# Moving the modulation sums of an adaptive-norm block out of the first attention and into the feed-forward and convolution stages

## What is computed

```python
x = x + attention(rmsnorm(x, attn_norm_g)) @ w_out           # 8 forgetting heads, 8 stick-breaking heads
u = causal_dwconv(rmsnorm(x, ffn_norm_g) @ w_up, conv_w, conv_b)
x = rmsnorm(x + (silu(gate(u)) * val(u)) @ w_down, final_norm_g)
sc = silu(c)
for i in range(2):
    mod = sc @ w_ada[i] + b_ada[i]                             # 1024 x 6144, for one row vector
    sh_m, sc_m, g_m, sh_f, sc_f, g_f = jnp.split(mod, 6, axis=-1)
    h = rms_norm(x, norm_mix[i]) * (1 + sc_m) + sh_m
    y = moba_attention(h) if i == 0 else short_conv(h, w_in, conv_w, w_out)
    x = x + g_m * y
    h = rms_norm(x, norm_ffn[i]) * (1 + sc_f) + sh_f
    x = x + g_f * swiglu(h, w_gate_up[i], w_down[i])
```

## Time and profile before

| | |
|---|---|
| median of 3 runs | 1031.73 us (1027.55 to 1032.73) |
| the profiled execution | 1032.79 us, of which the span is 1030.9 us |
| PE busy | 988.2 us, 96% of the span |
| DVE busy | 720.3 us, 70% |
| ACT busy | 484.0 us, 47% |
| mean granted TensorE clock | 0.969 |
| the 48 modulation steps on DVE (line 797) | 112.6 us, mean 2345 ns |

### The profile page before, as it was taken

One profiled execution on the slowest core, in us unless ns is written; L12 is line 12 of the kernel. 1 busy time (PEld: TensorE's weight loads), 2 busy tenths in 40 slices (PEclk: granted clock), 3 DMA queues, 4 the chain that ended last, 5 costly groups with the idle time before them and its releaser, 6 DMA issues.

```text
span 1030.9 us, 18959 instructions
## 1 busy us (share of the span) xinstructions
PE 988.2 (96%) x7553; PEld 959.3 (93%) x7553; DVE 720.3 (70%) x939; ACT 484.0 (47%) x696; POOL 45.2 (4%) x78
## 2 busy tenths in 40 slices
PE   5899987999999999999999999999999989999998
PEld 5899877999999999989999999999999989999876
DVE  5699884778788867888675677787666665555544
ACT  4245543556566334655454444433444454444531
POOL 4100000000000100001000001010000000000000
PEclk8999997999999997999989999999899999999999
DMA  9678473365554982646645688798265626455441
GB/s 319 219 234 304 173 264 110 111 196 163 174 195 170 385 300 60 227 163 222 231 131 194 211 284 279 247 365 283 91 198 168 199 85 201 165 197 169 165 162 41
DMA packets 131064, 207.60 MB, mean 201 GB/s; under 512 B 4686, under 2 KB 109504, under 8 KB 124864
## 3 DMA queue, kind: packets, MB, share of 16 engines
q1 hardware_dynamic: 122784, 156.44, 45.5%
q0 software_dynamic: 6912, 50.33, 13.8%
q10 hardware_dynamic: 1312, 0.04, 0.1%
HBM read 205.74 MB, written 1.05 MB: 201 GB/s over the span
## 4 chain that ended last, share of the span: by engine, by line
PE 85%; DVE 8%; ACT 3%; issue 2%; DMA 1%; SPq 1%; ACTq 0%; DVEq 0%
PE bank L1276 25%; PE bank L1277 25%; PE bank L1278 25%; PE bank L1356 2%; PE bank L1312 2%; DVE w_lo L782 2%; PE bank L1314 2%; PE bank L1317 1%; ACT w_hi L466 1%; SPq L377 1%; DMA v_in<-in_conv_w 1%; DVE ada_acc L797 1%; DVE scr L815 0%; ACT prob L727 0%; DMA k_fox<-sb_l 0%
## 5 line engine op out<-in xcount | busy, mean ns | idle before, releaser
L782 DVE TENSOR_TENSOR w_lo<-w_raw,w_hi 128x1024 fp32r<-128x1024 f32 x294 | 356.3, 1223 | 213.2 <-ACT w_hi L466 209.3
L466 ACT ACTIVATE w_hi<-w_raw 128x1024 fp32r<-128x1024 f32 x294 | 306.6, 1054 | 308.6 <-PE bank L1278 286.6
L1276 PE MATMUL bank<-act_hi,w_hi 128*128 128x256 f32 x1440 | 411.3, 286 | 1.1 <-DVE act_lo L1096 1.1
L1277 PE MATMUL bank<-act_lo,w_hi 128*128 128x256 f32 x1440 | 408.5, 284 | 0.0
L1278 PE MATMUL bank<-act_hi,w_lo 128*128 128x256 f32 x1440 | 408.4, 284 | 0.0
L1276 PEld LDWEIGHTS bank<-act_hi,w_hi 128*128 128x128 f32 x1440 | 276.3, 192 | 1.9 <-issue 1.7
L1277 PEld LDWEIGHTS bank<-act_lo,w_hi 128*128 128x128 f32 x1440 | 276.3, 192 | 0.3 <-issue 0.2
L1278 PEld LDWEIGHTS bank<-act_hi,w_lo 128*128 128x128 f32 x1440 | 276.1, 192 | 0.0
L797 DVE SCALAR_TENSOR_TENSOR ada_acc<-ada_raw,silu_c,ada_acc 128x2048 f32<-128x2048 f32 x48 | 112.6, 2345 | 2.2 <-DMA ada_raw<-in_w_ada 1.9
L1277 PE MATMUL bank<-hid_lo,w_hi 128*128 (+1 forms) x352 | 99.5, 283 | 0.0
L1276 PE MATMUL bank<-hid_hi,w_hi 128*128 (+1 forms) x352 | 99.2, 282 | 0.0
(11 more groups left out here) (248 smaller groups left out, 1297.5 us busy)
## 6 DMA issues: line engine op xcount, KB each, us to landing
ada_raw<-in_w_ada POOLq DMA_DIRECT2D x48, 1024.0 KB, 5.3
w_raw<-in_w_gate_up SPq DMA_DIRECT2D x44, 1024.0 KB, 5.1
w_raw<-in_w_down SPq DMA_DIRECT2D x33, 1024.0 KB, 5.0
w_raw<-in_w_in SPq DMA_DIRECT2D x24, 1024.0 KB, 5.3
w_raw<-in_w_up SPq DMA_DIRECT2D x22, 1024.0 KB, 5.1
w_raw<-in_w_qkv SPq DMA_DIRECT2D x12, 1024.0 KB, 7.0
w_raw<-in_w_out SPq DMA_DIRECT2D x8, 1024.0 KB, 5.2
w_raw<-in_w_o SPq DMA_DIRECT2D x4, 1024.0 KB, 5.9
```

The source lines that it names most:

```text
L466: act.activation(unit(w_hi, u), raw_half(c, h), ACT.Copy).then_inc(hi_ready, 1)
L782: dve.tensor_tensor(unit(w_lo, u), raw_half(c, h), unit(w_hi, u).bitcast(F32), ALU.subtract).then_inc(lo_ready, 1)
L1276: pe.matmul(dst, a_hi, b_hi, start=start, stop=False, skip_group_check=True)
L1277: pe.matmul(dst, a_hi, b_lo, start=False, stop=False, skip_group_check=True)
```

## The change

The 16 steps that stood in and behind the first attention are taken out of it, but for two that stand at its end. Six go into UP1 (pairs 1, 3, 4, 6, 8 and 9), the next eight into DOWN1, the following 24 into the second attention, UP2 and DOWN2, and the last eight into IN3, one behind each of its first eight chunks. The first two fetches of POOL move behind its fills of the padded tiles. `PIECES` gets an eighth piece, and three pieces (2, 4 and 6) are folded into the norms 4, 5 and 6, between `rstd` and the first use of the gain. On PE, the sums of piece 5 now stand between IN3 and OUT3. DVE's code for UP1 is written out for all 11 pairs instead of a loop.

```diff
-ADA_AT1 = [(1, 0), (1, 1), (2, 1), (3, 1), (4, 0), (4, 1), (5, 1), (6, 1), (7, 0), (7, 1), (9, 0), (10, 1), (11, 1),
-           (12, 0), (12, 1)]
+ADA_OUT1, ADA_UP1, ADA_IN3 = 2, (1, 3, 4, 6, 8, 9), 40
...
-PIECES = ((0, 0, 15), (0, 16, 31), (0, 32, 47), (1, 0, 15), (1, 16, 31), (1, 32, 39), (1, 40, 47))
+PIECES = ((0, 0, 15), (0, 16, 31), (0, 32, 39), (0, 40, 47), (1, 0, 15), (1, 16, 31), (1, 32, 39), (1, 40, 47))
+ACC_READ = (1, 2, 4)
...
                         for n in range(3):
                             pool.memset(ada_acc[:, n, :], 0.0).then_inc(ada_zero, 1)
-                        fetch(0)
-                        fetch(1)
...
                                 pool.memset(pad[64 * (1 - half):64 * (2 - half), half:8:2, :], value).then_inc(pad_set, 1)
+                        fetch(0)
+                        fetch(1)
...
                 link(dve.scalar_tensor_tensor(rstd[:], n_t[:], 1.5, n_y[:], ALU.add, ALU.mult))
+                if piece is not None:
+                    modulation(piece)
...
+                    if c0 == UP1 and p in ADA_UP1:
+                        ada(ADA_OUT1 + ADA_UP1.index(p))
                     gated_pair(c, pair, p, i, convolve)
...
-                    if (c, h) in ADA_AT1:
-                        ada(ADA_AT1.index((c, h)))
...
-            for n in range(len(ADA_AT1), 16):
+            for n in range(ADA_OUT1):
                 ada(n)
...
-            modulation(0)
-            gated_layer(UP1, 0, 1, True)
-            down_layer(DOWN1, 16, None)
+            gated_layer(UP1, 0, PAIRS, True)
+            down_layer(DOWN1, 8, None)
...
-            modulation(4)
             for c in range(12):
...
+                if c < 8:
+                    ada(ADA_IN3 + c)
             split(OUT3 + 2)
             split(OUT3 + 3)
+            modulation(5)
             add_up(OUT3, lambda k: mod[:, 1, G_M + k:G_M + k + 1])
-            modulation(5)
...
@@ PE @@
                 for h in range(2):
                     out1_chunk(n, h)
             square_sums(1)
-            mod_sums(0)
...
             square_sums(4)
+            mod_sums(2)
             mod_sums(3)
...
+            mod_sums(5)
             for n in range(4):
                 for h in range(2):
                     output_chunk(OUT3, n, h, lambda k: ot_hi[:, k, :], lambda k: ot_lo[:, k, :],
                                  lambda k: pe.wait_ge(sc_lo, k // 2 + 1) if k % 2 == 0 else None)
-            mod_sums(5)
             square_sums(6)
             mod_sums(6)
+            mod_sums(7)
```

More of the change, by code:

```diff
@@ L799, in _, with norm @@
             ada_step = [4]
-            def norm(n, gain, shift=None, version=None, late=None):
+            def norm(n, gain, shift=None, version=None, late=None, piece=None):
                 if late is not None:
@@ L906, in gated_layer @@
                     step(c0 + 2 * p, pair0 + p, p, None)
+                if straight == PAIRS:
+                    return
                 ada_step[0] = 2
@@ L1144, in _ @@
             split_unit(UP1 + 1, 1)
+            gated_layer(UP1, 0, PAIRS, True)
+            down_layer(DOWN1, 8, None)
+            norm(2, lambda k: vcol(0, V_FINAL + k), version=3, late=(QKV + 1, 0))
             modulation(0)
-            gated_layer(UP1, 0, 1, True)
-            down_layer(DOWN1, 16, None)
-            norm(2, lambda k: vcol(0, V_FINAL + k), version=3, late=(QKV + 1, 0))
-            modulation(1)
             norm(3, lambda k: gain2[:, 0, k:k + 1], shift=lambda k: mod[:, 0, SH_M + k:SH_M + k + 1])
             split_unit(QKV + 1, 1)
-            modulation(2)
+            modulation(1)
             def head_mean(n):
@@ L1219, in _ @@
             add_up(OUT2, lambda k: mod[:, 0, G_M + k:G_M + k + 1])
-            norm(4, lambda k: gain2[:, 1, k:k + 1], shift=lambda k: mod[:, 0, SH_F + k:SH_F + k + 1], late=(UP2 + 1, 0))
+            norm(4, lambda k: gain2[:, 1, k:k + 1], shift=lambda k: mod[:, 0, SH_F + k:SH_F + k + 1], late=(UP2 + 1, 0),
+                 piece=2)
             split_unit(UP2 + 1, 1)
             modulation(3)
-            gated_layer(UP2, PAIRS, 3, False, ADA + 8)
-            down_layer(DOWN2, ADA + 16, lambda k: mod[:, 0, G_F + k:G_F + k + 1])
-            norm(5, lambda k: gain2[:, 2, k:k + 1], shift=lambda k: mod[:, 1, SH_M + k:SH_M + k + 1], late=(IN3 + 1, 0))
+            gated_layer(UP2, PAIRS, 3, False, ADA)
+            down_layer(DOWN2, ADA + 8, lambda k: mod[:, 0, G_F + k:G_F + k + 1])
+            norm(5, lambda k: gain2[:, 2, k:k + 1], shift=lambda k: mod[:, 1, SH_M + k:SH_M + k + 1], late=(IN3 + 1, 0),
+                 piece=4)
             split_unit(IN3 + 1, 1)
-            modulation(4)
             for c in range(12):
@@ L1260, in _ @@
                                       ALU.subtract).then_inc(sc_lo, 1)
+                if c < 8:
+                    ada(ADA_IN3 + c)
             split(OUT3 + 2)
             split(OUT3 + 3)
+            modulation(5)
             add_up(OUT3, lambda k: mod[:, 1, G_M + k:G_M + k + 1])
-            modulation(5)
-            norm(6, lambda k: gain2[:, 3, k:k + 1], shift=lambda k: mod[:, 1, SH_F + k:SH_F + k + 1], late=(UP3 + 1, 0))
+            norm(6, lambda k: gain2[:, 3, k:k + 1], shift=lambda k: mod[:, 1, SH_F + k:SH_F + k + 1], late=(UP3 + 1, 0),
+                 piece=6)
             split_unit(UP3 + 1, 1)
-            modulation(6)
+            modulation(7)
             gated_layer(UP3, 2 * PAIRS, 1, False)
@@ L1639, in _ @@
             square_sums(2)
+            mod_sums(0)
+            square_sums(3)
             mod_sums(1)
-            square_sums(3)
-            mod_sums(2)
             def head_sums(n):
@@ L1651, in head_sums @@
                 else:
-                    pe.wait_ge(mod_done, 3)
+                    pe.wait_ge(mod_done, 2)
                 if n % 2 == 0:
```

4 lines of the change are left out of this document (2 added, 2 removed).

## The result

The changed kernel takes 1041.58 us (median of 4 runs, 1039.90 to 1044.52) against 1032.23 us (4 runs, 1027.55 to 1032.78): a ratio of 1.0119, 95% interval 1.0085 to 1.0152. It is slower: by 9.4 us between the medians, by 12 us by the ratio, whose interval is 8.8 to 15.7 us. The profiled execution took 1042.26 us, with a span of 1040.6 us and a mean granted clock of 0.966 (before 1030.9 and 0.969).

The account below looks back on a forecast made before the run. PE was taken as the bound, busy throughout UP1 and IN3, waiting little in the first attention. Added 10.0 us less 5.4 saved gave +4.6, stated as 1036.3 us; own range 1034 to 1039, 80% range 1030 to 1042.

Parts of the forecast that it names:

- the largest chance, 0.51: Whole kernel: chance given to a time the same as before, within about 0.5% (5.2 us).
- What the change takes away: First 184 us: four items (start, forget sums' wait, clock behind it, small waits) save 5.4 us.
- The start: Kernel start: small vectors land earlier with the fetches behind the fills, saving 0.8 us (bounds 0.5 and 1.05).
- the wait with its clock: First attention: PE's wait for the forget sums' moved rows goes, 2.3 us, and the half clock behind it, 1.2.
- The small waits: First attention: steps ahead of the first `o_tok` (0.4) and two `sb_t` (0.6, 0.2) go, taken as 1.1 us.
- The clock behind piece 5: Behind piece 5, after IN3: one-column products let PE's clock fall, costing 1.0 us (bounds 0 and 1.7).
- the clock holds: Rival, chance 0.15: piece 5 costs only its columns, with no clock loss, giving 1035.3 us.
- The second sums of norms 4 and 6 lie before the next `act_hi`: Norms 4 and 6: the second eight columns of sums end before `act_hi`, so no cost was added for them.
- The norms: Norms 4 and 6: the folded modulation between `rstd` and `scr` costs 0.5 us each.
- UP1 and IN3: Added steps make DVE late for PE: 2.0 us in UP1 (pairs 4 and 9, 1.0 each), 2.7 in IN3.
- DVE becomes the bound: Rival, chance 0.17: lateness carries on, UP1 costs 6.5 and IN3 5.6 us, +7.4, giving 1043.7 us.
- Norm 5: Norm 5: PE's 16 columns end late and the modulation follows, so `scr` comes 1.6 us later.

Follow-up runs that it names:

- e2: Kernel before with the accumulation at chunk (1, 0) taken out of the first attention, fetches unmoved: 1028.30 us, ratio 0.9971.
- e1: Kernel before with only POOL's first two 1 MB fetches moved behind its pad fills: 1027.41 us, ratio 0.9971.
- e11: Kernel before with 16 extra one-column products, the same as piece 5's, between IN3 and OUT3, result unused: 1039.49 us, ratio 1.0087.
- e12: Kernel before with eight extra f32 products of 256 columns between IN3 and OUT3, result unused: 1034.14 us, ratio 1.0043.
- e3: Changed kernel with UP1's six accumulations cut to 64 of 2048 columns, transfers unchanged: 1039.11 us, ratio 1.0080.
- e4: Changed kernel with IN3's eight accumulations cut to 64 of 2048 columns, transfers unchanged: 1037.08 us, ratio 1.0062.
- e5: Changed kernel with pieces 3 and 7 summed into bank 5 instead of bank 7: 1037.19 us, ratio 1.0067.
- e13: Changed kernel with the edits of e5 and e6, and UP1's six steps at pairs 0, 2, 4, 6, 8, 10: 1030.39 us, ratio 0.9995.
- e6: Changed kernel with piece 5 cut into four parts of four columns, ahead of the waits of IN3's chunks 6 to 9: 1033.98 us, ratio 1.0044.
- e7: Changed kernel with piece 5 cut into four parts of four columns, behind OUT3's first four half chunks: 1037.43 us, ratio 1.0076.
- e8: Kernel before with both small edits, later first fetches and no accumulation at chunk (1, 0): 1027.42 us, ratio 0.9975.

## Why the prediction was wrong

Its sign of the sum was right, its size was not: +4.6 us forecast, +9.7 in the profiled executions, 9.4 by the medians. The median, 1041.58 us, lies just inside the 80% range of 1030 to 1042 and outside the forecast's own 1034 to 1039, and the largest chance, 0.51, stood on a difference within 0.5%.

**What the change takes away** was read rightly. The start was 0.7 for 0.8 and the wait with its clock 4.1 for 3.5. e2 shows that the step at (1, 0) is the cause, as the forecast had it, and e1 that the fetches at the start act on the start alone. The small waits were 0.9 for 1.1 (the forecast's three terms of 0.4, 0.6 and 0.2 add up to 1.2): the one of 0.6 gave 0.9, the other two nearly nothing. Another 1.4 us is clock, which no step of the forecast held, and which is this pair of executions and not the change.

**The clock behind piece 5** is the step that failed. It took one stretch of 3.5 us from the earlier trace rows, bounded the loss by 1.7 and took 1.0. The changed kernel's own trace has 6.8 us at half clock there, which cost 1 us in the train (4.4 for 3.5) and 2.2 in OUT3, 3.2 us for the forecast's 1.0. e11 puts the train by itself at 7.8 us by the mean spans against 3.8 for e12's wide products, so at its columns and some 4 us of clock, of which its trace shows 3.1. The bound was one stretch where the changed kernel, e3 and e11 have two (e4 and e5 have one), and it left the train's own columns at full clock. The mechanism was right as far as it went: one-column products bring the clock down though PE stays busy. The rule of the Trainium skill (TensorE: Matmul & The Clock Gate, section "Part 1: The HAM clock gate"), which ties the full clock to a busy engine and warns of idle gaps, was weighed on the right side. These runs don't agree with it if "busy" is the profile's busy share: e11 and e12 keep PE busy without a gap, 4.00 of 4.00 us, and have clocks of 0.51 and 1.00. The rival "the clock holds" fell.

**"The second sums of norms 4 and 6 lie before the next `act_hi`"** was wrong. They wait for `mod_done` until 522.98, then run at half clock, and the chunk begins at 526.39. Behind `act_hi` it could have begun near 525.1, since in e5 it begins 1.05 us behind `act_hi`'s first row (524.50 in its timeline). The norms cost 1.0 and 1.7 us for 0.5 and 0.5; e5 gives back 1.0 us of the 1.7 that were missing. The forecast took the second eight columns at full clock (1.68 us); they began behind the wait and took 3.54 us at half clock.

**UP1 and IN3** were right in mechanism and small in size. In UP1 the two waits came where they were forecast (behind pairs 4 and 9) and cost the forecast's 1.0 us each; the other 1.0 us is 0.24 for each of the four steps that stand alone, which it put at nothing. IN3 cost 3.4 for 2.7, at chunks 7, 8 and 10. e3 and e4 show that it is DVE's time; e13 that neighbours make most of it in UP1. The rival that DVE becomes the bound (+7.4) did not come. **Norm 5** cost 2.4 for 1.6: the forecast took the 16 columns at 3.63 us, and in this execution they took 4.36, with the clock falling in them.

So against the forecast the loss is larger by 2.2 us at piece 5, 1.7 at norms 4 and 6, 1.0 in UP1, 0.8 in norm 5, 0.7 in IN3 and 0.4 between DOWN1 and OUT2, 6.8 together; the gain is larger by 1.7, most of it the clock of the two executions. That is the 5.1 us between +4.6 and +9.7. Without that luck on the side of the gain the forecast would have been off by more.

## What to carry to other kernels

A run of one-column products costs more than its rows say: it can halve TensorE's clock for the dense work behind it. Cut it into parts of a few columns and put these where TensorE waits anyway; here that was worth 6.5 us in the traces and 7.6 by the medians (e6 against the changed kernel). A step that moves into a stage where TensorE has no idle time is cheap only if the slower engine has caught up before the next one: in UP1 a step alone cost 0.24 us and one right behind another 1.0. So read the slack of one round, give each moved step a free round behind it, and look at what stands behind the last one too. And try the smallest part of a change by itself: leaving out the one step at (1, 0) gave 0.3%, where the whole change lost 1.2%.

## What the runs showed of the hardware

The same code has stretches at half clock in one execution and none in another. The changed kernel and e3 to e7 are alike up to 200 us; the changed kernel has the clock at 0.50 from 102.8 to 106.2 us, and so do e5 and e6 at 103 us, which costs each of the three 1.7 us that e3, e4 and e7 don't lose. 28 runs of the kernel before spread over 7.0 us (1027.10 to 1034.05), with mean clocks of 0.969 to 0.975, the low clocks in the long runs. One profiled execution therefore doesn't price a change of 2 or 3 us: e8's trace is 7.4 us ahead, its median 2.9. What could be read from single traces are the steps at one place, and what could be read from the medians is the sum.

Two 1 MB fetches on GpSimd's queue delayed the landing of the small vector rows on another queue by 3.4 us (PE turned them at 19.18, in e1 at 15.78), though the last of these loads is only 22 KB.
